# The experts' gate and up biases: from one row per turn to a table added by TensorE

## The chip, the cores and the metric

The kernel runs on one core of one Trainium2 chip. The metric is the device time of one execution in microseconds (us), the median of several runs. One execution of each kernel is also recorded with a profile; its times count from the start of the recorded span.

## What is computed

Two blocks run one after the other on 256 tokens of width 1024, all in f32. The first block (two layers of feed-forward, mixer, feed-forward) is untouched by the change. The second is a layer with attention and a mixture of 32 experts, each token going to 4 of them:

```python
h2 = rms_norm_2(x, norm2_g) * (1.0 + scale2) + shift2
# router: top 4 of 32, softmax over the four
gu = xe @ w_gate_up[e] + b_gate_up[e]          # 1024 -> 2048
g = jnp.minimum(gu[:, :1024], 7.0)
u = jnp.clip(gu[:, 1024:], -7.0, 7.0)
act = (u + 1.0) * (g * jax.nn.sigmoid(1.702 * g))
ye = act @ w_down[e] + b_down[e]               # 1024 -> 1024
x = x + gate2 * sum over the four experts of gate * ye
```

w_gate_up has 8 MB per expert and w_down 4 MB, so that the experts read 12 MB of weights 32 times.

## The kernel before

The program is written engine by engine: each phase is a block in which SyncE, GpSimd, TensorE (PE), ScalarE (ACT) and VectorE (DVE) each have their own order of instructions, joined by semaphores. Within an engine the written order holds.

**Weights.** Loads are issued by SyncE into a ring of six slots of 1 MB, in attention and before. In the expert phase six more slots join (`double`, `more`), so that a cycle is 12 slots, and transfers are of 2 MB, two slots each. Four extra slots (`once`) are used a single time, at expert 3 (APART). PE counts each slot it has consumed in `chip.used`, and SyncE waits for that count before it refills a slot (`emptied`). `landed` tells PE which count says that a slot is full.

**Experts** (`experts_phase`, from L2532). Each expert takes at most 64 tokens (CAP). The banks hold 128 rows: the 64 tokens times the first 512 columns in the lower half of the partitions, and times the last 512 columns in the upper half. Turn e on PE (`turn`) is `gate_up(e)` (eight slots, four products each, into GATE_BANK and UP_BANK, with the transposes `turn_back` after the fourth slot), `gather(e)` (tokens of expert e+1), `down(e)` (the hidden values of expert e-1 times its w_down, four slots), `turn_hidden(e)` and `scatter(e)` into four banks that stay open over all turns. Turn 0 has only gate_up and gathers, and two slots of gate_up(1) come before turn_hidden(0). Ahead of turn QUIET = 8, PE adds x and the down bias of all experts to the open banks (`add_x_and_bias`, L2741 to L2749).

**The bias before.** For each expert ScalarE issues an 8 KB DMA on its own queue (`bias_row`, L2779), which fills one partition; GpSimd spreads it over 128 partitions (`spread_bias`, L2658 to L2663). VectorE's `activate` (L2847) waits for both the products and the bias, adds it in four instructions of 64 rows each (L2852, L2857), clamps in two (L2861, L2864), multiplies by the sigmoid of ScalarE (L2797, L2866, L2869), and PE turns the result (L2727). `take_down` (L2876) scales the products of w_down.

**Attention** (`attend_phase`, L1688). PE multiplies in 24 `unit`s, whose weights ScalarE rounds (`lead`, L2009) and VectorE subtracts (`low`, L2178). ScalarE's order around the change is lead(23), evac(4), square_heads(3) (L2025), exps(3) (L2043), rms_heads(2) and (3) (L2029), take_w(2) (L2052). PE's is unit(21), pv(2) (L1864 to L1866), turn_w(3), unit(22), pv(3), unit(23), turn_heads(2). VectorE ends its part with norm_o(3), then the stt at L2396, and waits for the output product (L2401). SyncE's order is at L1735 to L1737: it waits for `x_final`, loads `norm2`, and goes on with the ring. `chip.norm_gb[:, 1, :]` is free from `x_final` on.

Of the kernel before, what the change touches and what calls it, by code (L numbers as in the profile page):

```python
# [78 lines left out]
class Chip:  # L79


    def __init__(self, nc, D, T):
        self.nc, self.D, self.T = nc, D, T
        self.KD, self.NT = D // P, T // P
        self.words = 53120
        words = 1900 + (2 * self.NT + 2) * D + self.KD * T + RING * SLOT
        self.memory = nc.alloc_sbuf_tensor("memory", [P, words], F32)
        self.psum = nc.alloc_psum_tensor("banks", [P, 8, 512], F32)
        w = Words(self.memory, 0, words)
        self.ident = w.take(P)  # L90
        self.incl = w.take(P)
# [3 lines left out]
        self.ident64, self.incl64, self.never = (w.take(64) for _ in range(3))  # L95
        self.gla_own = w.take(256)
        self.chunk_col = w.take(2)
        self.chunk_ones = w.take(2 * P).rearrange("p (c n) -> p c n", c=2)
        self.eps = w.take(4)
# [6 lines left out]
        self.xT = w.take(self.KD * T).rearrange("p (k t) -> p k t", k=self.KD)  # L106
        self.norm_gb = w.take(2 * D).rearrange("p (s d) -> p s d", s=2)
# [618 lines left out]
def mix_phase(chip, s, spent, l, loads, base, par, gamma_beta, skip, room, rows_before, mod_before):  # L726
# [72 lines left out]
    with nc.Block() as block:  # L799
# [509 lines left out]
        def _(dve):  # L1309
# [271 lines left out]
          "rank r_mm r_exp gates route_mm tables_turned gatesT")  # L1581
# [106 lines left out]
def attend_phase(chip, s, spent, routed, room, par, loads, base, n_project, b_down, mod_row, w_gate_up, w_down, rows_before):  # L1688
# [8 lines left out]
    gain2 = chip.norm_gb[:, 0, :]  # L1697
    SMALL = 4 + 8 + 4 + 3
# [16 lines left out]
    with nc.Block() as block:  # L1715
        @block.sync
        def _(sp):
# [18 lines left out]
            sp.dma_start(gain2, row(norm2)).then_inc(s["norm2"], 16)  # L1736
            chip.issue(sp, loads, base + RING + 4, OUT + RING)  # L1737
# [15 lines left out]
        def _(pool):  # L1753
# [14 lines left out]
            for m, fill in ((room.count, 0.0), (room.far, FAR)):  # L1768
                for a, n, start in ((0, P, 0), (P, 2 * P, P)):
# [8 lines left out]
                                 allow_small_or_imprecise_dtypes=True))  # L1778

# [220 lines left out]
        def _(act):  # L2000
# [120 lines left out]
            square_heads(3)  # L2121
            exps(3)
# [47 lines left out]
        def _(dve):  # L2170
# [222 lines left out]
            norm_o(3)  # L2393
            dve.wait_ge(s["norm2"], 16)
# [71 lines left out]
QUIET = 8  # L2466
ACC, GATE_BANK, UP_BANK, Y_BANK, SHARED_BANK = 0, 4, 5, 6, 7
EXPERTS = ("e_bias_row e_bias gu_read g_ready sig gated hidden sel back back_turned back_out gathered xe "
# [16 lines left out]
EXPERT_WORDS = 2048 + 1 + 2 * CAP + 256 + 256 + 3 * HALF + 2 * 8 * CAP + HALF + 3  # L2485
# [3 lines left out]
class ExpertRoom:  # L2489


    def __init__(self, chip, words, attend):
        self.double, self.more, self.once = attend.double, attend.more, attend.once
        w = Words(words, 0, EXPERT_WORDS)
        take3 = lambda a, b: w.take(a * b).rearrange("p (a b) -> p a b", a=a)
        self.bias_row, self.bias = w.take(2048), chip.norm_gb.rearrange("p s d -> p (s d)")
        self.idle = w.take(1)
# [30 lines left out]
BIAS_PIECES = 16  # L2528
# [3 lines left out]
def experts_phase(chip, s, spent, base, routed, room, gatesT, b_down, w_gate_up, b_gate_up, w_down, out):  # L2532
# [86 lines left out]
    with nc.Block() as block:  # L2619
# [36 lines left out]
        @block.gpsimd  # L2656
        def _(pool):
            def spread_bias(e):  # L2658
                pool.wait_ge(s["e_bias_row"], (e + 1) * 16)
                reach(pool, s["gu_read"], e)  # L2660

                nc.gpsimd.tensor_tensor(room.idle, chip.eps[:, 0:1], chip.eps[:, 1:2], ALU.add)
                nc.gpsimd.partition_broadcast(room.bias, room.bias_row[0:1, :]).then_inc(s["e_bias"], 1)  # L2663
# [112 lines left out]
        def _(act):  # L2776
            copy = nc.scalar.copy

            def bias_row(e):  # L2779
                reach(act, s["e_bias"], e)  # L2780
                act.dma_start(room.bias_row[0:1, :].rearrange("p (a n) -> p a n", a=BIAS_PIECES),
                              b_gate_up[0:1, ds1(e), :].rearrange("a e (k n) -> (a e) k n", k=BIAS_PIECES))\
                    .then_inc(s["e_bias_row"], 16)

# [19 lines left out]
            bias_row(0)  # L2804
            take_gathered(-1)
            bias_row(1)
# [3 lines left out]
            with act.Fori(1, NE - 1) as e:  # L2810
                take_back(e)
                bias_row(e + 1)
# [14 lines left out]
        def _(dve):  # L2827
# [18 lines left out]

            def activate(e):  # L2847
                dve.wait_ge(chip.used, taken(e, G8))
                dve.wait_ge(s["e_bias"], e + 1)
                reach(dve, s["turned"], e)  # L2850
                for h in range(2):
                    m = tt_op(room.gate[halves[h], :], psum[halves[h], GATE_BANK, :],  # L2852
                              room.bias[halves[h], h * HALF:h * HALF + HALF], ALU.add)
                m.then_inc(s["gated"], 1)
                for h in range(2):
                    c0 = D_EXPERT + h * HALF
                    m = tt_op(room.up[halves[h], :], psum[halves[h], UP_BANK, :], room.bias[halves[h], c0:c0 + HALF],  # L2857
                              ALU.add)
                    if h == 0:
                        dve.wait_ge(s["gated"], e * 2 + 1)  # L2860
                        ts(room.gate, room.gate, 7.0, None, ALU.min).then_inc(s["g_ready"], 1)  # L2861
                m.then_inc(s["gu_read"], 1)
# [4 lines left out]
                dve.wait_ge(s["gated"], e * 2 + 2)  # L2867
# [18 lines left out]
            gate2 = routed.gate2[:, 0:HALF]  # L2886
            select(-1)
# [153 lines left out]
def second_half(chip, s_attend, s_first, s_late, routed, par, loads, base, n_project, mod_row, w_gate_up, b_gate_up, w_down, b_down, out, rows_before):  # L3041

    nc = chip.nc
    with nc.sbuf_tensor("attend_words", [P, ATTEND_WORDS], F32) as words:
        with nc.sbuf_tensor("attend_parts", [P, PARTS_WORDS], F32R) as parts:
            pass
        with nc.sbuf_tensor("attend_later", [P, PARTS_WORDS], F32) as later:
            room = AttendRoom(chip, parts, later, words, routed)
            attend_phase(chip, s_attend, s_first.span(), routed, room, par, loads, base, n_project, b_down, mod_row, w_gate_up, w_down, rows_before)
# [86 lines left out]
```

## Time and profile before

| | us |
|---|---|
| median of 3 runs | 2338.59 (2338.49 to 2339.9) |
| the profiled execution | 2338.61 |
| its span | 2336.9 |
| PE busy | 2237.7 (96%) |
| DVE busy | 1050.3 (45%) |
| ACT busy | 598.0 (26%) |
| POOL busy | 173.3 (7%) |

Attention runs from about 1220 to 1377 us, the expert phase from there to the end. The page gives busy times by engine, the span in 40 slices, the DMA queues and the costliest groups. A group's line names the line of the code, the engine, the operation, what it writes and reads, and how often. PE products in plain f32 stand there with two records each, products of rounded operands with one. The chain of waits follows the work back from the last instruction; a timeline has each instruction's start and length, and in brackets the idle time before it and what ended that. DMA queue 1 is SyncE's, queue 10 ScalarE's.

### The profile page before, as it was taken

The numbers are of one execution on the slowest core, as the hardware profiler recorded it, in microseconds if no ns is written. First come the engines' busy times: TensorE is split into PE (matmuls) and PEld (weight loads), VectorE is DVE, ScalarE is ACT, GpSimd is POOL, SyncE is SP. The second block draws the span as 40 slices with busy tenths as digits, with TensorE's granted clock in tenths as the row PEclk, the third lists the DMA queues.
The fourth block names the chain that finished last, engine by engine and source line by source line (L and its number), as shares of the span: only waits on it lengthen the run. The fifth ranks groups of instructions, "written<-read, shape, count | busy, mean of one in ns | idle before, by whom it ended". The sixth has DMA issues, their size and how long they took to land. (4 is left out here: it accounts for less than half of the span.)

```text
span 2336.9 us, 31286 instructions
## 1 busy us (share of the span) xinstructions
PE 2237.7 (96%) x12797; PEld 1408.6 (60%) x12798; DVE 1050.3 (45%) x1497; ACT 598.0 (26%) x809; POOL 173.3 (7%) x194
## 2 busy tenths in 40 slices
PE   7999989999999998999999999999999999999998
PEld 6886875788788776668877654444443333333333
DVE  4563573665566447556558642222222222222222
ACT  4442331543443322244436521000000000000000
POOL 5000020000000001000010001000100000000000
PEclk9999999999999999999999999999999999999999
DMA  8763311687387352158635659999999999999996
GB/s 276 246 237 105 124 74 45 226 271 244 108 282 248 116 164 77 38 168 281 235 128 168 226 225 423 399 425 411 424 426 425 425 428 423 407 417 407 412 425 254
DMA packets 189376, 633.61 MB, mean 271 GB/s; under 512 B 29568, under 2 KB 125840, under 8 KB 163392
## 3 DMA queue, kind: packets, MB, share of 16 engines
q1 hardware_dynamic: 189216, 631.96, 70.7%
q8 instruction: 73, 1.20, 0.2%
q10 hardware_dynamic: 64, 0.26, 0.0%
q14 instruction: 23, 0.19, 0.0%
HBM read 631.12 MB, written 1.07 MB: 271 GB/s over the span
## 5 line engine op out<-in xcount | busy, mean ns | idle before, releaser
L403 PE MATMUL banks<-ffn_room 128*128 128x512 f32 x1920 | 453.7, 392 | 0.0
L403 PEld LDWEIGHTS banks<-ffn_room 128*128 128x128 f32 x1920 | 357.5, 188 | 72.8
L520 DVE TENSOR_TENSOR ffn_room<-memory,ffn_room 128x2048 fp32r<-128x2048 f32 x124 | 280.9, 2292 | 99.2 <-ACT ffn_room L480 99.1
L2852 DVE TENSOR_TENSOR attend_words<-banks,memory 64x512 f32<-64x512 f32 x64 | 44.2, 690 | 529.6 <-PE banks L2682 529.2
L480 ACT CAST ffn_room<-memory 128x2048 fp32r<-128x2048 f32 x124 | 232.0, 1903 | 69.0 <-PE banks L421 61.9
L421 PE MATMUL banks<-ffn_room 128*128 128x512 f32 x1056 | 248.2, 390 | 0.3
L421 PEld LDWEIGHTS banks<-ffn_room 128*128 128x128 f32 x1056 | 197.6, 188 | 42.8 <-DVE ffn_room L559 2.1
L2682 PE MATMUL banks<-attend_later,attend_words 128*64 128x512 f32 x960 | 217.7, 595 | 3.1 <-DMA attend_later<-in_w_gate_up 2.3
L2698 PE MATMUL banks<-memory,attend_words 128*64 128x512 f32 x952 | 211.4, 595 | 0.0
L2682 PE MATMUL banks<-attend_words 128*64 128x512 f32 x496 | 122.6, 640 | 28.5 <-DMA attend_words<-in_w_gate_up 28.3
L2682 PEld LDWEIGHTS banks<-attend_later,attend_words 128*64 128x64 f32 x960 | 66.1, 136 | 129.5 <-issue 122.4
L2698 PEld LDWEIGHTS banks<-memory,attend_words 128*64 128x64 f32 x952 | 65.0, 135 | 121.1 <-issue 117.6
L2717 PEld LDWEIGHTS banks<-attend_words,memory 128*128 128x128 f32 x1056 | 120.5, 192 | 26.0 <-issue 26.0
L2682 PE MATMUL banks<-memory,attend_words 128*64 128x512 f32 x592 | 134.2, 597 | 0.7 <-ACT attend_words L2793 0.7
L2717 PE MATMUL banks<-attend_words,memory 128*128 128x64 f32 x1056 | 124.8, 276 | 0.0
L486 ACT ACTIVATE memory<-banks 128x256 f32<-128x256 f32 x88 | 33.8, 385 | 342.6 <-PE banks L403 318.8
L2793 ACT COPY attend_words<-banks 128x512 f32<-128x512 f32 x33 | 19.4, 587 | 392.1 <-PE banks L2717 392.1
L535 DVE TENSOR_TENSOR memory<-memory,banks 128x256 f32<-128x256 f32 x88 | 36.8, 418 | 176.7 <-ACT memory L486 166.0
L2682 PEld LDWEIGHTS banks<-attend_words 128*64 128x64 f32 x496 | 36.3, 146 | 112.1 <-issue 67.3
L869 PE MATMUL banks<-memory 128*128 128x400 f32 (+1 forms) x256 | 101.1, 549 | 1.2 <-PEq L363 1.2
L2663 POOL PARTITION_BROADCAST memory<-attend_words x32 | 73.9, 2309 | 289.3 <-issue 289.3
L2682 PEld LDWEIGHTS banks<-memory,attend_words 128*64 128x64 f32 x592 | 39.3, 135 | 89.2 <-issue 88.4
(434 smaller groups left out, 2398.9 us busy)
## 6 DMA issues: line engine op xcount, KB each, us to landing
memory<-in_ffn_w SPq DMA_DIRECT2D x132, 1024.0 KB, 7.5
memory<-in_w_down SPq DMA_DIRECT2D x58, 2048.0 KB, 23.2
attend_later<-in_w_gate_up SPq DMA_DIRECT2D x58, 2048.0 KB, 24.3
memory<-in_w_gate_up SPq DMA_DIRECT2D x34, 2048.0 KB, 22.0
attend_words<-in_w_gate_up SPq DMA_DIRECT2D x30, 2048.0 KB, 24.7
memory<-in_w_in SPq DMA_DIRECT2D x32, 1024.0 KB, 6.3
memory<-in_w_ada SPq DMA_DIRECT2D x32, 768.0 KB, 5.6
memory<-in_w_out SPq DMA_DIRECT2D x12, 1024.0 KB, 4.9
```

The costliest lines, as they stand in the source:

```text
L403: m = nc.tensor.matmul(psum[:, GU + tt, :], x_parts[:, xp, k, tt * P:tt * P + P], rows, start=(n == 0), stop=(n == 3 * KD - 1))
L421: return nc.tensor.matmul(psum[:, 2 * tt + h, :], hidden_parts[:, ft % 2, hp, tt, c, :], rows[:, c, h * 512:h * 512 + 512], start=(ft == 0 ...
L480: nc.scalar.copy(split_place(i)[0], chip.ring[:, chip.slot(base + i), :]).then_inc(s["lead"], 1)
L486: nc.scalar.activation(gate[:, tt, :], psum[:, GU + tt, 0:FT], ACT.Silu).then_inc(s["gate"], 1)
L520: tt_op(b, chip.ring[:, chip.slot(base + i), :], a.bitcast(F32), ALU.subtract).then_inc(chip.used, 1)
L535: tt_op(hidden[:, tt, :], gate[:, tt, :], psum[:, GU + tt, FT:2 * FT], ALU.mult)\
L869: m = mm(psum[:, n % 2, 0:cols], chip.xT[:, k, half * P:half * P + P], slots[k // 4][:, k % 4, :], start=(k == 0), stop=(k == KD - 1))
L2663: nc.gpsimd.partition_broadcast(room.bias, room.bias_row[0:1, :]).then_inc(s["e_bias"], 1)
L2682: m = mm(psum[halves[h], bank, :], room.xeT[:, k, :], rows[:, c0 + h * HALF:c0 + h * HALF + HALF], start=(k == 0), stop=(k == G8 - 1))
L2698: m = mm(psum[halves[h], Y_BANK, :], room.actT[:, k, :], rows[:, c * D_EXPERT + h * HALF:c * D_EXPERT + h * HALF + HALF], start=(k == 0), ...
L2717: m = mm(psum[:, SHARED_BANK, k * CAP:k * CAP + CAP], routed.h2[:, tt, k * P:k * P + P], room.sel[:, tt, :], start=(tt == 0), stop=(tt == ...
L2852: m = tt_op(room.gate[halves[h], :], psum[halves[h], GATE_BANK, :], room.bias[halves[h], h * HALF:h * HALF + HALF], ALU.add)
```

## The change

The biases of all experts are loaded once, in attention, into one table of 128 partitions and 2 x 512 columns: partitions 0 to 31 hold the first half of the gate and up columns of experts 0 to 31, 32 to 63 the second half, and 64 to 127 the same again. ScalarE rounds the upper copy to the type f32r (`bias_table`, partitions 0 to 63) and the lower likewise (`bias_low`), and VectorE puts the remainder of the rounding into partitions 64 to 127. GpSimd prepares two small masks. In the experts VectorE makes a 128x128 selector for each expert (`pick`), and PE adds the bias by one product with that selector into each of the two banks, ahead of the weight products, which then add on. The per-turn row, the broadcast and the four additions are gone; VectorE clamps straight from the banks. QUIET becomes 18, so that x and the down bias are added ahead of turn 18.

```diff
-QUIET = 8
+QUIET = 18
@@ attend_phase, SyncE
             sp.dma_start(gain2, row(norm2)).then_inc(s["norm2"], 16)
+            for r in range(0, P, NE):
+                sp.dma_start(bias_raw[r:r + NE, :].rearrange("e (g n) -> e g n", g=2),
+                             b_gate_up[0:1, :, :].rearrange("a e (g h n) -> (a e) h g n", g=2, h=2)[:, (r // NE) % 2, :, :])\
+                    .then_inc(s["bias"], 16)
             chip.issue(sp, loads, base + RING + 4, OUT + RING)
@@ attend_phase, GpSimd, after its last step
+            chain(nc.gpsimd.memset(chip.bias_rows[:, NE:NE + 1], 0.0))
+            chain(nc.gpsimd.memset(chip.bias_halves, 0.0))
+            for i in range(P // NE):
+                chain(nc.gpsimd.memset(chip.bias_halves[i * NE:i * NE + NE, CAP * (i % 2):CAP * (i % 2) + CAP], 1.0))
...
@@ attend_phase, ScalarE
             square_heads(3)
+            act.wait_ge(s["bias"], 16 * (P // NE))
+            act.wait_ge(s["bias_made"], 1)
+            copy(chip.bias_table[halves[0], :], bias_raw[halves[0], :]).then_inc(s["bias_lead"], 1)
+            act.wait_ge(s["bias_lead"], 1)
+            copy(chip.bias_low[halves[1], :], bias_raw[halves[1], :]).then_inc(s["bias_lead"], 1)
             exps(3)
@@ attend_phase, VectorE
             norm_o(3)
+            dve.wait_ge(s["bias_lead"], 2)
+            tt_op(chip.bias_table[halves[1], :], bias_raw[halves[1], :], chip.bias_low[halves[1], :].bitcast(F32), ALU.subtract)
             dve.wait_ge(s["norm2"], 16)
@@ experts_phase, GpSimd
-            def spread_bias(e):
...
-            spread_bias(0)
-            with pool.Fori(1, NE) as e:
-                spread_bias(e)
@@ experts_phase, TensorE, gate_up
                 reach(pe, s["gu_read"], e)
+                if tiles[0] == 0:
+                    pe.wait_ge(s["picked"], e + 1)
+                    for g, bank in enumerate((GATE_BANK, UP_BANK)):
+                        mm(psum[:, bank, :], room.pick, room.bias[:, g, :],
+                           start=True, stop=True)
                 for k in tiles:
...
-                                   rows[:, c0 + h * HALF:c0 + h * HALF + HALF], start=(k == 0), stop=(k == G8 - 1))
+                                   rows[:, c0 + h * HALF:c0 + h * HALF + HALF], start=False, stop=True,
+                                   skip_group_check=True)
@@ experts_phase, ScalarE
-            bias_row(0)
             take_gathered(-1)
-            bias_row(1)
...
                 take_back(e)
-                bias_row(e + 1)
                 take_gathered(e)
@@ experts_phase, VectorE
+            def pick(e):
+
+                ts(room.pick, room.halves, room.rows[:, ds1(e)], None, ALU.mult).then_inc(s["picked"], 1)
+
             def activate(e):
                 dve.wait_ge(chip.used, taken(e, G8))
-                dve.wait_ge(s["e_bias"], e + 1)
                 reach(dve, s["turned"], e)
-                for h in range(2):
-                    m = tt_op(room.gate[halves[h], :], psum[halves[h], GATE_BANK, :],
-                              room.bias[halves[h], h * HALF:h * HALF + HALF], ALU.add)
...
-                ts(room.up, room.up, 7.0, -7.0, ALU.min, ALU.max)
+                ts(room.gate, psum[:, GATE_BANK, :], 7.0, None, ALU.min).then_inc(s["g_ready"], 1)
+                ts(room.up, psum[:, UP_BANK, :], 7.0, -7.0, ALU.min, ALU.max).then_inc(s["gu_read"], 1)
+                pick(e + 1)
                 dve.wait_ge(s["gu_read"], e + 1)
...
+            pick(0)
             select(-1)
```

The table, the selector and the masks lie in memory that the first block's mixer used for constants and, for the table, next to `norm_gb`; nothing else moves.

## Rows read from the trace of the kernel before

**Rows 1.** The page: busy times of the engines, and the DMA row in 40 slices.
```profile
PE 2237.7 (96%) x12797; PEld 1408.6 (60%) x12798; DVE 1050.3 (45%) x1497; ACT 598.0 (26%) x809; POOL 173.3 (7%) x194
...
DMA  8763311687387352158635659999999999999996
```

**Rows 2.** Table of stretches: span, busy of PE, PEld, DVE, ACT, POOL, clock, DMA, GB/s.
```profile
1600.00:1620.00 20.00, 20.00 (x76) 6.29 (x78) 0.00 (x0) 0.37 (x1) 0.00 (x0) 1.00 0.94 383
...
1700.00:1720.00 20.00, 19.79 (x108) 9.00 (x106) 9.05 (x13) 1.71 (x3) 2.66 (x2) 1.00 1.01 431
...
2000.00:2304.00 304.00, 286.45 (x1420) 116.21 (x1420) 75.91 (x130) 20.84 (x40) 26.63 (x20) 0.98 1.00 414
```

**Rows 3.** Chain of waits in order of time: start us, us, what.
```profile
1542.03 7.02 PE banks L2682 x32
...
1567.22 0.70 DVE attend_words L2876
...
1569.96 7.02 PE banks L2682 x32
...
1597.88 8.43 PE banks L2749 x16
...
2000.34 5.38 PE banks L2682 x16
...
2304.83 3.65 PE banks L2682 x16
```

**Rows 4.** Timeline of SyncE, turn 3 to 4.
```profile
1469.27 3.76 SPq L2633 DMA_DIRECT2D memory<-in_w_down  x2
1489.96 0.36 SPq L2633 DMA_DIRECT2D memory<-in_w_gate_up  x1
```

**Rows 5.** DMA view, 1485 to 1493: busy tenths in 40 slices.
```profile
DMA  9939937935335313113113113113099960098199
```

**Rows 6.** DMA view of 1525.3 to 1526.3, then issues of three later stretches.
```profile
q10 hardware_dynamic: 1, 0.01, 2.0%
...
attend_words<-in_b_gate_up ACTq DMA_DIRECT2D x10, 8.0 KB
...
attend_words<-in_b_gate_up ACTq DMA_DIRECT2D x8, 8.0 KB
...
memory<-in_w_down SPq DMA_DIRECT2D x20, 2048.0 KB, 24.3
...
attend_words<-in_b_gate_up ACTq DMA_DIRECT2D x9, 8.0 KB
```

**Rows 7.** PE's waits from 1731 to 2305: in total, times, longest.
```profile
PE banks L2682 <- DMA attend_words<-in_w_gate_up: 28.3, 16, 2.8
```

**Rows 8.** Timeline of PE in turn 0.
```profile
1405.19 0.66 PE L2727 MATMUL banks<-memory,attend_words 128*128 128x128 f32 x4 [0.16 <-DVE attend_words L2869]
```

**Rows 9.** Rounded and plain f32 products of 512 columns: page's group, then timeline.
```profile
L403 PE MATMUL banks<-ffn_room 128*128 128x512 f32 x1920 | 453.7, 392 | 0.0
...
1317.88 3.68 PE L1894 MATMUL banks<-memory 128*128 128x512 f32 x8
```

**Rows 10.** Timelines of SyncE and ScalarE in attention.
```profile
1256.95 2.51 SPq L132 DMA_DIRECT2D memory<-in_w_in  x2
...
1286.56 1.04 ACT L2009 CAST attend_parts<-memory 128x1024 fp32r<-128x1024 f32 x1 [1.97 <-PE banks L1812]
```

**Rows 11.** Timelines of ScalarE, PE and VectorE around the added steps.
```profile
1295.45 1.05 ACT L2009 CAST attend_parts<-memory 128x1024 fp32r<-128x1024 f32 x1 [0.70 <-PE banks L1812]
...
1301.99 0.77 ACT L2052 COPY attend_words<-banks 128x768 f32<-128x768 f32 x1
...
1302.82 0.43 PE L1864 MATMUL banks<-attend_words 128*128 128x64 f32 x2 [1.29 <-ACT attend_words L2052]
...
1357.10 1.22 DVE L2401 TENSOR_TENSOR memory<-attend_later,banks 128x1024 f32<-128x1024 f32 x1 [5.51 <-PE banks L1894]
```

**Rows 12.** Table of stretches (columns as in rows 2).
```profile
1302.00:1306.00 4.00, 3.18 (x20) 3.09 (x21) 2.48 (x10) 1.22 (x3) 0.00 (x0) 0.80 0.34 139
```

More of the change, by code:

```diff
@@ L86, in __init__ @@
         words = 1900 + (2 * self.NT + 2) * D + self.KD * T + RING * SLOT
+        at = -(-nc.sbuf_base // 32) * 32
         self.memory = nc.alloc_sbuf_tensor("memory", [P, words], F32)
+        self.rounded = nc.alloc_sbuf_tensor_at("memory_rounded", [P, words], F32R, offset=at)
         self.psum = nc.alloc_psum_tensor("banks", [P, 8, 512], F32)
@@ L90, in __init__ @@
         self.ident = w.take(P)
+        self.bias_low = self.rounded[:, w.at:w.at + D]
         self.incl = w.take(P)
@@ L95, in __init__ @@
         self.ident64, self.incl64, self.never = (w.take(64) for _ in range(3))
+        self.bias_pick = self.rounded[:, w.at + 64:w.at + 192]
         self.gla_own = w.take(256)
@@ L106, in __init__ @@
         self.xT = w.take(self.KD * T).rearrange("p (k t) -> p k t", k=self.KD)
+        self.bias_table = self.rounded[:, w.at + D:w.at + 2 * D]
         self.norm_gb = w.take(2 * D).rearrange("p (s d) -> p s d", s=2)
@@ L1580 @@
           "d_ss d_rms d_out mix_turned mixT mixed x_new x_turned n_ss n_rms hT_first hT_last cst_mm shifted "
-          "rank r_mm r_exp gates route_mm tables_turned gatesT")
+          "rank r_mm r_exp gates route_mm tables_turned gatesT bias bias_lead bias_made")
 class Routed:
@@ L1685, with attend_phase @@
 PIECES = ((0, P), (P, WIDE))
-def attend_phase(chip, s, spent, routed, room, par, loads, base, n_project, b_down, mod_row, w_gate_up, w_down, rows_before):
+def attend_phase(chip, s, spent, routed, room, par, loads, base, n_project, b_down, mod_row, w_gate_up, b_gate_up, w_down, rows_before):
     nc, D, KD, NT = chip.nc, chip.D, chip.KD, chip.NT
@@ L1697, in attend_phase @@
     gain2 = chip.norm_gb[:, 0, :]
+    bias_raw = chip.norm_gb[:, 1, :]
     SMALL = 4 + 8 + 4 + 3
@@ L2465 @@
 CAP = 64
-QUIET = 8
+QUIET = 18
 ACC, GATE_BANK, UP_BANK, Y_BANK, SHARED_BANK = 0, 4, 5, 6, 7
-EXPERTS = ("e_bias_row e_bias gu_read g_ready sig gated hidden sel back back_turned back_out gathered xe "
+EXPERTS = ("picked gu_read g_ready sig gated hidden sel back back_turned back_out gathered xe "
            "turned act ye scat down_bias tables scat_first first_rows last_rows")
@@ L2495, in __init__ @@
         take3 = lambda a, b: w.take(a * b).rearrange("p (a b) -> p a b", a=a)
-        self.bias_row, self.bias = w.take(2048), chip.norm_gb.rearrange("p s d -> p (s d)")
-        self.idle = w.take(1)
+        self.bias = chip.bias_table.rearrange("p (g n) -> p g n", g=2)
+        self.pick, self.halves, self.rows = chip.bias_pick, chip.bias_halves, chip.bias_rows
         self.sel = take3(chip.NT, CAP)
@@ L2657, in _ @@
         def _(pool):
-            def spread_bias(e):
[L2659 to L2663, printed above, removed]
             pool.sem_clear(spent)
-            spread_bias(0)
-            with pool.Fori(1, NE) as e:
-                spread_bias(e)
         @block.tensor
@@ L2777, in _ @@
             copy = nc.scalar.copy
[L2779 to L2783, printed above, removed]
             def take_back(e):
@@ L2845, in select_back @@
                 m.then_inc(s["back"], 1)
+            def pick(e):
+                ts(room.pick, room.halves, room.rows[:, ds1(e)], None, ALU.mult).then_inc(s["picked"], 1)
             def activate(e):
                 dve.wait_ge(chip.used, taken(e, G8))
-                dve.wait_ge(s["e_bias"], e + 1)
                 reach(dve, s["turned"], e)
-                for h in range(2):
-                    m = tt_op(room.gate[halves[h], :], psum[halves[h], GATE_BANK, :],
-                              room.bias[halves[h], h * HALF:h * HALF + HALF], ALU.add)
[L2854 to L2862, printed above, removed]
+                ts(room.gate, psum[:, GATE_BANK, :], 7.0, None, ALU.min).then_inc(s["g_ready"], 1)
+                ts(room.up, psum[:, UP_BANK, :], 7.0, -7.0, ALU.min, ALU.max).then_inc(s["gu_read"], 1)
+                pick(e + 1)
                 dve.wait_ge(s["gu_read"], e + 1)
-                ts(room.up, room.up, 7.0, -7.0, ALU.min, ALU.max)
                 dve.wait_ge(s["sig"], e + 1)
                 tt_op(room.gate, room.gate, room.sig, ALU.mult).then_inc(s["gated"], 1)
-                dve.wait_ge(s["gated"], e * 2 + 2)
+                dve.wait_ge(s["gated"], e + 1)
                 by_row = lambda v: v.rearrange("p (n c) -> p c n", c=4)
@@ L3048, in second_half @@
             room = AttendRoom(chip, parts, later, words, routed)
-            attend_phase(chip, s_attend, s_first.span(), routed, room, par, loads, base, n_project, b_down, mod_row, w_gate_up, w_down, rows_before)
+            attend_phase(chip, s_attend, s_first.span(), routed, room, par, loads, base, n_project, b_down, mod_row, w_gate_up, b_gate_up, w_down, rows_before)
             experts_phase(chip, s_first, s_late.span(), base + n_project + N_OUT, routed, ExpertRoom(chip, words, room), room.gatesT, room.b_down,
```

5 lines of the change are left out of this document (3 added, 2 removed).

## The prediction

> **What bounds the kernel now.** I read the page first. PE is busy 96% of the span, and the DMA row in tenths stands at 9 from slice 24 on, so from about 1400 us two resources are full at once [rows 1]. The table of stretches tells them apart. From 1700 to 1720 PE is busy 19.79 of 20 us; from 2000 to 2304 it is busy 286.45 of 304 us, so it waits, and the sixteen DMA engines carry 414 to 431 GB/s all along, with shares of 0.99 to 1.01 [rows 2]. The chain of waits has the same turning point. A turn of the expert loop takes 27.93 us while PE leads it (1542.03 to 1569.96); late in the loop the waits for weights at 2000.34 and 2304.83 are ten turns apart, 30.45 us each [rows 3]. An expert's weights are 12.58 MB, which at 426 GB/s take 29.5 us. PE is thus faster per turn than the transfers, and the stock of landed slots is used up on the way.
>
> So the end is set by a sum of three: when the stream of weights can start, what it loses when slots come free too late, and how fast it runs. Two places of loss are seen. At 1489.96 SyncE issues a load after a gap of some 17 us (the two before it went out from 1469.27 on) [rows 4]: ring slots are short there, since the four extra ones are used once, and the load waits for PE's second product group of turn 4. The DMA row of 1485 to 1493 (slices of 0.2 us) falls from 9 to 3 and then 1 before it rises at 1490.8 [rows 5]. I read that as follows: the sixteen engines don't run dry together; the first ends at about 1486, the last not before 1491, so after 100 us of streaming they are 4 to 5 us apart, and a transfer has landed only when its slowest engine is done. The other place is 1600 to 1620, at 383 GB/s instead of 426 [rows 2], behind the 8.43 us of x and down bias [rows 3].
>
> **Part 1, the bias rows go.** In 1490 to 1757, 1757 to 2000 and 2000 to 2304 the ACT queue issues 10, 8 and 9 rows of 8 KB, 27 in all [rows 6]. In the microsecond from 1525.3 queue 10 has one data packet, which takes 2.0% of sixteen engines' time: 0.02 x 16 = 0.32 us on one engine. At 426 / 16 = 26.6 GB/s the 8192 bytes would take 0.31 us, so the whole row lies on one engine [rows 6]. By mean throughput that is 0.02 us a turn and nothing. But if that engine is the slowest, each turn loses 0.31 us, 27 x 0.31 = 8.4 us. The ends are 0 and 8.4; I take nine tenths, 7.6, nearer to the upper end, since the spread of the engines at 1485 to 1493 shows that one engine decides and this one alone has work added.
> The row shows one packet on one engine, not which engine nor whether it is always the same. The Trainium skill (DMA: Bandwidth & Descriptors, section Why a DMA increments its semaphore by 16 and not by 1) states that a DMA from the scalar queue which can't be divided goes to the lowest-numbered engine; by that all rows add up on one engine and the upper end holds; were they dealt round, the saving would be 0.5 us. No view of the profile numbers the engines, so the trace neither agrees nor disagrees.
>
> GpSimd's broadcast and VectorE's four 64-row additions per turn go too. In the late turns neither is in the chain, where VectorE appears only with take_down's 0.70 us [rows 3]; PE's waits late in the loop are for transfers (28.3 us in 16) [rows 7]. Worth: 0. In turn 0 VectorE's product of the gates does end a wait of 0.16 us of PE, which the next part uses up [rows 8].
>
> **Part 2, two products per expert.** Full-width single-record products of this shape in the feed-forward took 453.7 us for 1920, 0.236 each [rows 9]. So 2 x 0.236 = 0.47 us a turn on PE, at the start of gate_up, before the products that free slots. A turn of PE becomes 28.4 us, still under the transfers' 30. The upper end: the plain f32 calls of the output projection are two records each, 3.68 us for 8 records, 0.92 a call [rows 9], 1.84 us a turn if the rounded type did not hold; the change reads both operands through the rounded view, so I take 0.47. A gain is excluded: the weight products stay the same. Up to the load of 1489.96 five pairs come (turns 0 to 4): 5 x 0.47 = 2.35, less the 0.16 in turn 0, is 2.2 us later. There the last engine is running dry just as the new load begins to move (about 1 us after its issue), so up to about half a microsecond of lateness is free; I charge 1.7 (1.2 to 2.2). After the restart the pairs cost nothing, PE having 1.6 us a turn to spare over the transfers; that cover gone, each would cost 0.47. In turn 31 the pair runs while PE would wait for the last weights. VectorE's pick of 128 columns lies behind the two clamps, long before the next expert's products.
>
> **Part 3, x and down bias from turn 8 to turn 18.** At turn 8 the stock is thin and the engines with a lead run dry: 383 for 426 GB/s over 20 us is 2.0 us of mean throughput [rows 2]. The slowest engine hardly stops, for the reason read at 1485 to 1493. Value 0, ends -2.0 and 0. At turn 18 the same 8.43 us meet queued transfers worth some 24 us (issue to landing in the last window is 24.3 us [rows 6]), so nothing stops; PE is then late by 8.4 and regains 30 - 28.4 = 1.6 us a turn, in six turns of the thirteen left. Cost 0; if PE's turn were near 30, it would not be regained.
>
> **Part 4, the table in attention.** SyncE issues four loads of 128 KB behind norm2's. The next load in its queue is a w_in slot, issued from 1256.95 on, whose first reader is ScalarE's cast at 1286.56 [rows 10], so about 2.5 us of issue is covered; 0.5 MB is 1.2 us of transfer in a stage with the queues half empty [rows 1]. GpSimd's masks are small and stand after its last counted step; queue and engine are idle there. Cost 0.
> ScalarE is given two copies of 64x1024 between square_heads(3) and exps(3), at 1298.4. A cast of 1024 columns takes 1.05 us, for 128 rows and I take the same for 64 [rows 11]; two with the wait between them 2.1. Queued behind are exps(3), rms_heads and take_w(2) (L2052, 1301.99), and for take_w(2) PE waits already: 1.29 us of idleness before its product at 1302.82 [rows 11]. So all of it goes to the path: +2.1, from there through pv(2), units 22 and 23 and turn_heads, which stand in PE's order. From below, 1.0 if ScalarE's own idle time took one copy; from above 3.4, if PE's longer pause costs it more time at half clock: from 1302 to 1306 the granted clock was 0.80 already [rows 12].
> VectorE's subtraction of 64x1024 (1.2 us) lies in the 5.51 us that it idles before 1357.10 [rows 11]: 0.
>
> **Sum.** Against the profiled execution's own 2338.61 (span 2336.9 and 1.7 around it; the median of the runs is 2338.59, the same): -7.6 + 1.7 + 0 + 2.1 = -3.8, so 2334.8 us. About 0.2%, 4.7 us, is what a measurement can tell from no change; the forecast lies just within.
>
> **Rivals.**
> A, the rows' engine isn't the slowest, or rows are dealt round: 27 x 0.02 = 0.5 instead of 7.6 gives 2338.6 - 0.5 + 1.7 + 2.1 = 2341.9. For it: the mean throughput hardly notices the rows. Against: the engines' spread. 0.12.
> B, all of the row's price comes back, and the pause at turn 8 counts too: -8.4 - 2.0 + 1.7 + 2.1 = 2332.0; with quieter neighbours on the engines somewhat less. For it: the drop to 383 GB/s is plain in the windows. 0.37.
> C, slower: the products cost as plain f32, 1.84 a turn. Then the restart comes 5 x 1.84 - 0.16 - 0.5 = 8.5 us late, PE's turn is 29.8, and the 8.43 us at turn 18 are regained at 0.3 a turn, 4 of them in thirteen turns, 4.4 left: 2338.6 + 2.1 + 8.5 + 4.4 - 7.6 = 2346.0. It decides from a PE turn of about 29.5 us on, a pair of 1.6. With a longer half-clock stretch in attention (+1.3) on top of rival A it would reach 2343.2 in another way. Together 0.13.
> D, the change doesn't do what it says for the path, since every removed step is covered: that is A.
> The forecast has 0.38.
>
> **How the numbers follow.** Faster by over 0.2% (under 2333.9): B, 0.37, and 0.03 of the forecast's lower edge: 0.40. Slower (over 2343.3): C, 0.13. Same: the rest, 0.47. The range goes from B's 2332.0 less the quieter neighbours and ScalarE's lower end (3 us) to A with its clock cost: 2329 to 2343.5.
>
> **What the profile would show.** Right: no queue 10 and no broadcast; the chain's late turns at 30.1 to 30.2 us; SyncE's load of 1489.96 at 1494.3; PE's pause before L1864 at 3.4 instead of 1.29; PE turns of 28.4 before the waits begin; no dip at 1600 to 1620; the tail behind the last weights still 32 us. Late turns unchanged at 30.4 would speak for A; pairs at over 1.6 us for C. The prediction would be wrong if packets of the weights themselves changed speed once the ACT queue is silent, which no row of before can show.

## The result, and the profile after

The changed kernel takes 2315.24 us (median of six runs, 2313.12 to 2317.9) where the kernel before takes 2338.54 (six runs, 2336.37 to 2339.9): a ratio of 0.9902, 95% interval 0.9889 to 0.9914. That is 23.3 us, or 1.0%, off; 3.8 had been forecast, and the result lies well under the range of 2329 to 2343.5. The profiled execution of after took 2313.12 us with a span of 2311.4. One execution of the kernel before, among the 13 beside group 2 below, took 4608.56 us, and the ratios leave it out.

The page of after, answering to [rows 1]:
```profile
PE 2246.0 (97%) x12861; PEld 1418.9 (61%) x12862; DVE 973.5 (42%) x1403; ACT 600.2 (26%) x811; POOL 89.7 (4%) x137
...
DMA  8773311677386343139745559899999999999998
```
Its table of stretches (columns as in rows 2), the experts' chain, and the chain's shares by engine over the whole span:
```profile
1600.00:1620.00 20.00, 19.79 (x101) 8.31 (x101) 2.69 (x8) 0.96 (x2) 0.00 (x0) 1.00 1.01 430
...
2000.00:2304.00 304.00, 301.70 (x1528) 125.02 (x1527) 52.27 (x105) 22.81 (x44) 0.00 (x0) 1.00 0.98 419
```
```profile
1602.29 0.66 PE banks L2692 x2
1602.95 7.02 PE banks L2699 x32
...
1631.54 7.02 PE banks L2699 x32
```
```profile
PE 39%; DVE 1%; issue 0%; ACT 0%
```
PE is busy 301.70 of 304 us late in the loop, where it was 286.45 [rows 2]. A turn takes 1631.54 - 1602.95 = 28.59 us (28.58 in the mean of ten) with the pair of products (L2692) in it, and no transfer is in the chain. PE's waits from 1731 to 2305 have one line left where a transfer's 28.3 us stood [rows 7]:
```profile
PE banks L2755 <- DVE attend_words L2878: 4.1, 20, 0.2
```
So the bound has changed hands: before, the transfers set a late turn (30.4 us), now PE does (28.58). The stretch 1600 to 1620 moves 430 GB/s instead of 383.

Attention of after, answering to rows 11 and 12, timelines of ScalarE and PE, then a stretch:
```profile
1294.39 1.03 ACT L2140 CAST memory_rounded<-memory 64x1024 fp32r<-64x1024 f32 x1
1295.45 1.05 ACT L2142 CAST memory_rounded<-memory 64x1024 fp32r<-64x1024 f32 x1
```
```profile
1300.95 0.69 PE L1880 MATMUL banks<-attend_words 128*128 128x64 f32 x2 [3.44 <-ACT attend_words L2068]
```
```profile
1302.00:1306.00 4.00, 4.00 (x18) 3.81 (x18) 2.13 (x7) 0.80 (x1) 0.00 (x0) 0.50 0.02 4
```
The two copies cost PE 3.44 - 1.29 = 2.15 us of waiting, and the granted clock behind it is 0.50 (1.2 GHz) where it was 0.80.

One more difference stands at the very start, where the change touches nothing. GpSimd and PE in the first microseconds, of before and then of after:
```profile
11.73 0.28 POOL L633 TENSOR_SCALAR_AFFINE_SELECT memory<-memory 128x128 f32<-128x128 f32 x1 [10.69 <-issue]
12.16 3.65 PE L653 MATMUL banks<-memory 128*128 128x128 f32 x16 [12.16 <-POOL memory L633]
```
```profile
1.29 0.29 POOL L639 TENSOR_SCALAR_AFFINE_SELECT memory<-memory 128x128 f32<-128x128 f32 x1 [0.24 <-POOL memory L638]
6.20 3.67 PE L659 MATMUL banks<-memory 128*128 128x128 f32 x16 [6.20 <-DMA memory<-in_x]
```
Before, GpSimd idles 10.69 us for nothing that the profile shows ("issue"), and PE's first product waits for it. The same kind of gap stands in each turn of the expert loop of before, between the idle addition and the broadcast (timeline of GpSimd, then its waits from 1377 on):
```profile
1652.02 0.35 POOL L2662 TENSOR_TENSOR attend_words<-memory 128x1 f32<-128x1 f32 x1 [15.48 <-DVE attend_words L2857]
1662.16 2.30 POOL L2663 PARTITION_BROADCAST memory<-attend_words  x1 [9.79 <-issue]
```
```profile
POOL memory L2663 <- issue: 289.3, 32, 10.8
```
32 gaps, 289.3 us, 9.0 us each. The addition waits for VectorE before it starts; between it and the broadcast no semaphore stands, and still 9 us pass. These rows carry the explanation below.

### The profile page after: what moved, and what is told of

It reads as the page before. It is cut to its first block and busy times, and to the rows that moved or that the text cites. A ratio compares the mean times of both kernels' runs of the same rounds, so it can differ in the third digit from the quotient of the medians.

```text
span 2311.4 us, 30925 instructions
## 1 busy us (share of the span) xinstructions
PE 2246.0 (97%) x12861; PEld 1418.9 (61%) x12862; DVE 973.5 (42%) x1403; ACT 600.2 (26%) x811; POOL 89.7 (4%) x137
## 5 line engine op out<-in xcount | busy, mean ns | idle before, releaser
L2863 DVE TENSOR_SCALAR attend_words<-banks 128x512 f32<-128x512 f32 x32 | 22.1, 692 | 518.7 <-PE banks L2699 518.7
L2699 PE MATMUL banks<-attend_words 128*64 128x512 f32 x496 | 111.8, 592 | 0.0
L2800 ACT COPY attend_words<-banks 128x256 f32<-128x256 f32 x32 | 11.9, 373 | 305.6 <-PE banks L2726 305.6
L871 PE MATMUL banks<-memory 128*128 128x256 f32 x384 | 85.4, 379 | 0.0
```

The source lines that it names most:

```text
L871: m = mm(psum[:, n % 2, c * 256:c * 256 + 256], slots[k // 4][:, k % 4, cc:cc + P], chip.xT[:, k, :], start=(k == 0), stop=(k == KD - 1))
L2699: m = mm(psum[halves[h], bank, :], room.xeT[:, k, :], rows[:, c0 + h * HALF:c0 + h * HALF + HALF], start=False, stop=True, skip_group_chec ...
```

## The experiments

Four theories stood: rows (8 KB on one DMA engine each turn), writing (what GpSimd's broadcast puts into memory, 1 MB a turn, disturbs the transfers), switching (the idle addition and the broadcast are taken to be different code on GpSimd, and each change of code disturbs the transfers; no view shows the code itself, so "change of code" stands below for an addition followed by a broadcast, or a broadcast by an addition), and the move of the 8.43 us of x and down bias. The kernels ran in four groups, each beside the kernel before, whose medians were 2337.43 (16 runs), 2339.16 (13), 2336.59 (15) and 2338.18 us (15); differences of 1 us between groups mean nothing. The ratios are taken over all runs and not from the two medians, and can differ from their quotient by as much as 1 us.

**Group 1: parts undone one by one, in the kernel before.** The row loaded for expert 0 alone (both later calls of `bias_row` gone, the broadcast kept); the broadcast for expert 0 alone:
```diff
-                pool.wait_ge(s["e_bias_row"], (e + 1) * 16)
+                pool.wait_ge(s["e_bias_row"], 16)
...
-                bias_row(e + 1)
```


> The kernel before, with ScalarE's bias row loaded for expert 0 alone; the broadcasts, VectorE's additions and turn 8 stay (all experts but the first get the wrong bias). Rows theory (the 8 KB rows on ScalarE's queue are what slows the weight stream, by 0.31 us a turn on one engine and by slowed packets of the others): late turns fall from 30.4 to 29.3 us, the time to 2312 to 2320. Broadcast theory (GpSimd's broadcast disturbs the transfers): 2330 to 2337, the 8.4 us of the rows at most. Turn-8 theory (the pause at turn 8 is what costs): 2336 to 2339.

```diff
-                nc.gpsimd.tensor_tensor(room.idle, chip.eps[:, 0:1], chip.eps[:, 1:2], ALU.add)
-                nc.gpsimd.partition_broadcast(room.bias, room.bias_row[0:1, :]).then_inc(s["e_bias"], 1)
+                m = nc.gpsimd.tensor_tensor(room.idle, chip.eps[:, 0:1], chip.eps[:, 1:2], ALU.add)
+                if isinstance(e, int) and e == 0:
+                    m = nc.gpsimd.partition_broadcast(room.bias, room.bias_row[0:1, :])
+                m.then_inc(s["e_bias"], 1)
```


> The kernel before, with GpSimd's broadcast for expert 0 alone, the rows still loaded each turn (all experts but the first get the wrong bias). Rows theory: 2336 to 2339, late turns 30.4 us. Broadcast theory: late turns 29.5 us, 2312 to 2322. Turn-8 theory: 2336 to 2339.

Both edits together, and `QUIET` set to 18 with nothing else changed:

> The kernel before with neither rows nor broadcasts after expert 0 (all experts but the first get the wrong bias). Rows and broadcast theories alike: late turns 29.3 us, 2308 to 2318, and equal to whichever of the two single removals is the cause. If the layout of memory or the products are the cause, 2330 to 2339.

> The kernel before with QUIET = 18 alone, output complete. Rows and broadcast theories: 0 to 2 us faster, 2336 to 2339, since the slowest DMA engine hardly stops at turn 8 and the late turns stay at 30.4 us. Turn-8 theory: 2315 to 2330.

| kernel | us | against the before of its group | ratio, 95% |
|---|---|---|---|
| no rows | 2329.06 | -8.4 | 0.9966 (0.9955 to 0.9978) |
| no broadcasts | 2314.23 | -23.2 | 0.9905 (0.9889 to 0.9922) |
| neither | 2309.08 | -28.4 | 0.9881 (0.9864 to 0.9897) |
| bias at turn 18 | 2337.07 | -0.4 | 0.9999 (0.9989 to 1.0009) |

The move is worth nothing, though its stretch 1600 to 1620 shows 428 GB/s instead of 383. The broadcasts alone are worth as much as the whole change. The rows bring more than the broadcast theory had left for them (2330 to 2337) and far less than the rows theory asked for (2312 to 2320). The late turns tell the same by the turn; each pair of lines is the chain of one kernel, nine turns apart: before, no rows, no broadcasts, neither.
```profile
2005.86 24.77 DMA attend_words<-in_w_gate_up
...
2279.07 25.71 DMA attend_words<-in_w_gate_up
```
```profile
1968.21 25.51 DMA attend_words<-in_w_gate_up
...
2239.14 26.62 DMA attend_words<-in_w_gate_up
```
```profile
1987.28 25.62 DMA attend_words<-in_w_gate_up
...
2254.23 25.48 DMA attend_words<-in_w_gate_up
```
```profile
1984.27 25.50 DMA attend_words<-in_w_gate_up
...
2248.59 25.48 DMA attend_words<-in_w_gate_up
```
30.36, 30.10, 29.66 and 29.37 us a turn. The row is worth 0.26 (beside broadcasts) or 0.29 (without); the broadcast 0.70 or 0.73. The figures with broadcasts are the rough ones: single turns of before scatter there from 28.2 to 32.7 us (13 turns from 1882.34 on make 30.52 in the mean), while without rows and broadcasts each is within 0.03 of 29.37.

**Group 2: what of the broadcast costs.** First, the kernel before with the idle addition left out and GpSimd's loop written out, so that 32 broadcasts stand one behind the other:
```diff
-                nc.gpsimd.tensor_tensor(room.idle, chip.eps[:, 0:1], chip.eps[:, 1:2], ALU.add)
...
-            spread_bias(0)
-            with pool.Fori(1, NE) as e:
+            for e in range(NE):
                 spread_bias(e)
```


> The kernel before, complete, with GpSimd's one-element addition ahead of each broadcast left out and its loop written out, so that GpSimd runs nothing but broadcasts. Switching theory (what slows the packets is the preparation of some 9 us between that addition and the broadcast, in which GpSimd changes from built-in to loaded code): the gap before the broadcasts is gone, late turns are 29.6 to 29.7 us and the time is that of the kernel without broadcasts, 2312 to 2318. Writing theory (the broadcast's own 1 MB of writes into SBUF slows the packets): late turns 30.4 us, 2335 to 2339.

2319.82 us (2318.15 to 2320.08), ratio 0.9923 (0.9905 to 0.9941). The gaps are gone from GpSimd's waits, which are:
```profile
POOL memory L2662 <- DVE attend_words L2855: 798.9, 31, 33.9
POOL memory L2662 <- issue: 139.5, 1, 139.5
```
Late turns take 29.69 us by its chain, as with no broadcasts at all:
```profile
1993.28 25.82 DMA attend_words<-in_w_gate_up
...
2260.47 25.51 DMA attend_words<-in_w_gate_up
```
The median is 5.6 us longer than without broadcasts all the same, and above the 2312 to 2318 of the switching theory; the turns don't account for it.

Then the other way round, added to the changed kernel: in each turn the addition and a broadcast of 16 columns (8 KB written), or two additions of 128x1024 on GpSimd (1 MB written, no change of code), or the row on ScalarE's queue.
```diff
+                nc.gpsimd.tensor_tensor(room.idle, chip.eps[:, 0:1], chip.eps[:, 1:2], ALU.add)
+                nc.gpsimd.partition_broadcast(room.spare[:, 0:16], chip.x[0:1, 0, 0:16]).then_inc(s["e_bias"], 1)
```


> The kernel after, output complete, with one addition and a broadcast of only 16 columns (8 KB instead of 1 MB) per expert on GpSimd, whose result nobody uses. Switching theory: the packets are slowed as in the kernel before, late turns 30.1 us and waits for transfers come back: 2328 to 2336. Writing theory: no effect, 2313 to 2318.

```diff
+                for h in range(2):
+                    reach(pool, s["e_bias"], e * 2 + h)
+                    nc.gpsimd.tensor_tensor(room.spare, chip.x[:, h, :], chip.x[:, 1 - h, :], ALU.add).then_inc(s["e_bias"], 1)
```


> The kernel after, output complete, with two additions of 128x1024 per expert on GpSimd (1 MB of writes, no broadcast), whose result nobody uses. Switching theory: no effect, 2313 to 2318. Writing theory: transfers slowed as before, 2328 to 2336. A third, that GpSimd's use of the port it shares with VectorE delays VectorE enough to reach PE: PE's waits for L2878 grow from 7.2 us in all.

```diff
+                act.dma_start(room.bias_row[0:1, :].rearrange("p (a n) -> p a n", a=16),
+                              b_gate_up[0:1, ds1(e), :].rearrange("a e (k n) -> (a e) k n", k=16))\
+                    .then_inc(s["e_bias_row"], 16)
```


> The kernel after, output complete, with the 8 KB row per expert on ScalarE's queue put back, its data unused. Row theory (0.31 us a turn on the slowest engine): the transfers need 29.6 us a turn instead of 29.3 while PE needs 28.6, so part of it shows: 0 to 4 us slower, 2315 to 2319. If the row alone slowed all packets, 2325 or more.

The small broadcast took the changed kernel back to 2336.62 us (2333.84 to 2339.97; ratio to before 0.9994, 0.9984 to 1.0004), with the gaps back in GpSimd's waits:
```profile
POOL memory L2686 <- issue: 315.2, 32, 11.2
```
The large additions left it at 2315.02 (2314.61 to 2317.71), and PE's waits for VectorE's `take_down` stayed at 7.2 us in all, so the third theory, of the port, fails too. The row made it 2320.89 (2319.9 to 2324.04), beyond the 2315 to 2319 expected. So the writing costs nothing measurable, additions and broadcasts in turn cost 21 us, and the row 5.6.

**Group 3: the start, the layout of the row, the copies.** The 5.6 us that the unswitched kernel had too much point at the start: every kernel whose last GpSimd instruction is a broadcast shows the gap of some 10 us at its start. If an execution starts with the code that the one before it left, an addition behind the last broadcast should end that.
```diff
                 spread_bias(e)
+            pool.wait_ge(s["e_bias"], NE)
+            nc.gpsimd.tensor_tensor(room.idle, chip.eps[:, 0:1], chip.eps[:, 1:2], ALU.add)
```


> The kernel before, complete, with one more addition of one column on GpSimd behind the last broadcast, so that GpSimd ends the program on built-in code instead of broadcast code. In the profile of before GpSimd's L633 starts at 11.73 us, 10.69 us late for nothing that the profile shows, and TensorE's first product waits for it until 12.16; in the profile of the changed kernel the same instruction starts at 1.29 and the first product at 6.2, for a transfer. Theory S (an execution begins with the code that the last one left, and must bring the built-in code back): L633 starts at about 1.3, the first product at about 6.2, attention 4 to 5 us earlier, and the time is about 2334 (2332 to 2335.5), with the 31 switches of the experts' loop left as they are. Rival N (the late start is chance, or belongs to the program's length): 2337 to 2340, L633 at about 11.7.

> The kernel before, complete, without the idle addition in each turn of GpSimd's stream (its loop written out, so that 32 broadcasts follow each other with no built-in code between them) and with one addition behind the last of them. With the broadcasts alone it took 2319.8 us and its first product started at 12.22. Theory S (the first experiment of this call): the first product at about 6.2 and 2314 to 2316. If so, all 32 broadcasts of 8 KB and all 32 row loads are there, and what is gone of before is only the changing of code: 1 + 31 times. It would be about as fast as the changed kernel, so the products, the attention table and the moved biases bring nothing by themselves beside it. Rival N: 2319 to 2321.

In both the first select is at 1.52 us and the first product at 6.05 and 5.90, here for the kernel before with the addition:
```profile
1.52 0.29 POOL L633 TENSOR_SCALAR_AFFINE_SELECT memory<-memory 128x128 f32<-128x128 f32 x1 [0.49 <-POOL memory L632]
...
6.05 3.47 PE L653 MATMUL banks<-memory 128*128 128x128 f32 x16 [6.05 <-DMA memory<-in_x]
```
The unswitched kernel went from 2319.82 to 2314.4 (2312.81 to 2317.9), as expected. The kernel before went from 2336.59 only to 2335.62 (ratio 0.9997, 0.9988 to 1.0006; some -2.8 to +1.4 us): the instructions moved as expected, the time did not.

The copies of the table moved behind `take_w(3)` (the diff is shortened), and the row of group 2 laid out over 16 partitions:
```diff
             exps(3)
             rms_heads(2)
             rms_heads(3)
             take_w(2)
             take_w(3)
+            (the two copies of the bias table)
```


> The changed kernel, complete, with the copies of the bias table on ScalarE in attention moved behind the exps and scalings of heads 2 and 3, away from the wait that TensorE has at L1880. In the profile of the changed kernel that wait is 3.44 us where it was 1.29, and the products behind it run at a granted clock of 0.50 for a while. Theory: both go, 2.1 us of waiting and about 1.3 us of clock: 2311 to 2313. Rival (ScalarE is late again for the next reader of the same chain, so the copies only move the wait): 2314 to 2316.

> The changed kernel with the 8 KB row of gate and up biases loaded again each turn on ScalarE's queue and read by nobody, but laid out over 16 partitions, 512 bytes each. With the row as one partition it took 2320.9 (5.6 us over the changed kernel), its packets lying on few of the 16 DMA engines. Theory E (the row costs by what it adds to the slowest engine, 0.3 us a turn): spread out, it adds a sixteenth to each, and the time is 2315 to 2317. Rival Q (a second queue beside the weights costs by itself, whatever its layout): 2320 to 2322.

Moved, PE's wait before L1880 is the old 1.29 us again (timeline of PE):
```profile
1299.01 0.43 PE L1880 MATMUL banks<-attend_words 128*128 128x64 f32 x2 [1.29 <-ACT attend_words L2068]
```
The experts' first products stand 2.9 us earlier (1380.18 for 1383.08), and the time is 2310.91 us (2307.89 to 2313.91; ratio to before 0.9889, 0.9874 to 0.9904), the shortest complete kernel of this study. The spread row took 2316.92 (2316.06 to 2319.95) where the row on one partition took 2320.89. By their ratios the two are 3 us apart and the intervals overlap (0.9933, 0.9914 to 0.9953, and 0.9920, 0.9907 to 0.9934); the chains are clearer: the last turns that wait for transfers take 29.61 us with the row on one partition and 29.37 with the spread one, which is the figure without any row. The pages have queue 10 so, one partition first:
```profile
q10 hardware_dynamic: 64, 0.26, 0.0%
```
```profile
q10 hardware_dynamic: 1024, 0.26, 0.1%
```
That is 2 and 32 packets a row. The code cuts the row on one partition into 16 pieces too (`a=16` in the diff of group 2), and it went out undivided all the same. So what the row costs is mostly that it lies on one engine.

**Group 4: how the terms add.**

> The changed kernel, complete, with one addition of one column and one broadcast of 16 columns on GpSimd at the start of the experts' stage and nothing on GpSimd behind them, so that the program ends on broadcast code and changes code once in the loop. Theory S (the next execution's start pays for that): GpSimd's first affine select at about 12 us instead of 1.29, TensorE's first product at about 12.2 instead of 6.2, attention 4 to 5 us later, and, since TensorE and not the transfers bounds this kernel's experts, the whole of it at the end: 2319 to 2321. Rival N (a late start is made good later, as the 2335.6 of the kernel before with one more addition at its end would have it): 2315 to 2317, the first product late all the same.

> The changed kernel, complete, with the addition and the 16-column broadcast in each turn, and one more addition behind the last, so that 31 changes of code stay in the loop and none is left for the next start. Without the last addition it took 2336.6. Theory S as a plain sum: 4.5 to 5.5 us less, 2331 to 2332.5. Theory S with a floor (when the changes of code hold the transfers back, an earlier start of TensorE is mostly lost in waiting for them): 2334 to 2336.5, and TensorE waits more for transfers than without the addition.

> The changed kernel without the two products a turn that add the gate and up biases (these biases are left out of the result; the table is still loaded and copied in attention). In the profile of the changed kernel a turn of TensorE takes 28.58 us, and 27.93 in the profile of before. Theory P (TensorE's turns set the end): 0.65 us a turn less, 2315.2 minus 20 would be 2295. Theory F (the transfers move 428 to 429 GB/s, their most, and stand just behind TensorE, so that with TensorE faster they set the end at 29.3 to 29.4 us a turn): 2310 to 2314, TensorE waiting for transfers in the last ten turns.

One broadcast at the start of the experts and no addition behind it: 2318.1 us (2315.91 to 2320.5), 2.9 over the changed kernel, between what the two theories gave. Its start is late like that of before:
```profile
11.57 0.28 POOL L639 TENSOR_SCALAR_AFFINE_SELECT memory<-memory 128x128 f32<-128x128 f32 x1 [10.54 <-issue]
12.00 3.65 PE L659 MATMUL banks<-memory 128*128 128x128 f32 x16 [12.00 <-POOL memory L639]
```
Addition and broadcast in every turn and a start without the gap: 2335.56 (2332.96 to 2340.45), so the loop's changes alone are 20.3 us over the changed kernel, and the start brings 1.1 beside them. That is the time of the theory with a floor, but not its reason: PE waits no longer for transfers than without the last addition (18.1 and 18.3 us in all), and attention begins only 0.8 us earlier (1216.17 for 1217.00). Without the products: 2311.07 (2310.72 to 2312.23), 4.2 off instead of 20; the chain's late turns are
```profile
2046.26 25.49 DMA attend_words<-in_w_gate_up
...
2251.81 25.50 DMA attend_words<-in_w_gate_up
```
seven turns of 29.36 us. That is the transfers' floor for this loop, with nothing else on the engines. The changed kernel, at 28.58 a turn, runs on the stock of landed slots and comes to its end just before the stock does: in the kernel with the copies moved, which is 2.9 us earlier in the loop, one wait for a transfer (at 2254.65) is back in the chain.

## Why the prediction was wrong, step by step

**The step that failed** is the sentence "Worth: 0" on GpSimd's broadcast in part 1. It asked whether broadcast or addition was in the chain of waits; neither was, and that was right. The wrong step was to take from this that nothing else on the chip paid for them. The trace of before had 32 gaps of 9 us between an addition and a broadcast with no semaphore between them, and one of 10.69 us at the start, and none was asked about. Taken away, they are worth, in the loop, 20.3 us (the changed kernel with and without them) and 0.70 to 0.73 us a turn (the late turns), and at the start 1 to 5.4 us by kernel. The prediction's last sentence named the outcome (the weights' packets change speed) but held the ACT queue responsible; with the rows gone and the broadcasts kept it was 8.4 us, not 23.
That the alternation, and not the writing, slows the transfers is shown by the 8 KB broadcast with an addition (+21) against 1 MB of additions (0), and by the broadcasts without additions (late turns 29.69). The traces also show where in a turn it happens. Mean GB/s over the 22 broadcasts from 1625 to 2280, in stretches counted from each broadcast's start:

| kernel | 6 to 2 us before | 2 before to 6 behind | 6 to 10 behind | 10 to 16 behind |
|---|---|---|---|---|
| before | 407 | 427 | 389 | 428 |
| no rows | 421 | 429 | 401 | 428 |
| broadcasts without additions | 428 | 428 | 429 | 428 |

So there are two dips. One lies in the 9 us gap between addition and broadcast; the other behind the broadcast, where GpSimd waits for VectorE and no gap is seen. That the way back has a gap of its own shows only where an addition follows a broadcast at once: in the kernel before with one more addition at the end, that addition starts after 11.2 us of "issue". The sixteen engines are busy in the dips (shares of 0.99 to 1.00), so the packets take longer there. By the bytes missing in the two dips, the loss is about 0.56 us a turn in before and 0.33 in the kernel without rows (estimates from the table), of the 0.70 to 0.73 that the turns show. What it is on the chip that slows the packets isn't shown: the page counts no more data on any queue with the alternation than without. The Trainium skill (GPSIMD Engine Reference, section 2.1, Instruction dispatch) says that new code can be brought in to GpSimd by DMA at run time and that the first call to freshly loaded code pays about 6 us that no instruction shows. The gaps are of that kind, and here they measure 9.0 us in the mean, before every broadcast that follows an addition; that these two instructions differ in this way is inferred, not seen.

**The rows** were costed at 7.6, ends 0 and 8.4. Undone alone they are worth 8.4 (interval 5.1 to 10.5; late turns 30.10, where 30.1 to 30.2 had been named), added to the changed kernel 5.6. The reasoning by one slow engine held: the row spread over 16 costs 1.7. The rows add up, at 0.26 to 0.29 us a turn for a packet of 0.31, so they fall on one and the same engine; the Trainium skill's rule of the lowest-numbered engine (DMA: Bandwidth & Descriptors, section Why a DMA increments its semaphore by 16 and not by 1) fits that, though no view shows which engine it is. Rival A is out.

**The products** were put at 0.47 us a turn; the pair takes 0.66 in the chain and a turn grew from 27.93 to 28.58, 0.65. The rounded type held (rival C is out), but the row it was taken from has 0.236 a product and these take 0.33. The larger slip is "after the restart the pairs cost nothing": with turns of transfers at 30.4 that was so; at 29.36 the pair brings PE close to the transfers, and it costs 4.2 us (1.7 had been charged); it does not cost 31 x 0.65 = 20, since without it the transfers set the end. The restart load came at 1492.41 for 1494.3: attention began 4.0 us earlier, its clock took 1.3 and five pairs 0.9 more than was charged.

**The move of x and down bias**: 0, and 0 was measured (-0.4, interval -2.6 to +2.1). The dip to 383 GB/s goes and brings nothing.

**Attention** was put at +2.1, upper end 3.4. PE's pause was 3.44 as said. From GpSimd's first mark of attention to the experts' first products it is 1383.08 - 1214.43 = 168.65 us, before 1383.02 - 1218.45 = 164.57; less the new pair's 0.66 that is +3.4, the upper end. The 1.3 beyond the pause is put down to the lower clock behind it; with the copies moved both are gone (164.85).

**The start** wasn't in the sum at all. Attention begins at 1214.43 instead of 1218.45. Over all profiled kernels it begins at 1217.0 to 1223.3, mean 1219.8, in the six whose last GpSimd instruction is a broadcast, and at 1214.4 to 1218.8, mean 1215.9, in the eleven others: 3.9 us of the 6 that the first product gains.

Put together: without rows and broadcasts, -28.4 us; the products give back 4.2, and with about 1 for the rest -23.3 is what remains. That 1 is a remainder and was not measured by itself; in the changed kernel, where PE sets the end, moving the copies alone gave 2.4 to 4.3 us. The single terms (8.4 and 23.2) add to 3.2 more than their 28.4 together, which is within their intervals.

**What stays open** is what in the change between addition and broadcast slows the packets, and how much of the early start reaches the end while transfers set it: 1.0 and 1.1 us in the two kernels with changes in the loop, 2.9 and 5.4 in those without, each known to about 2 us.

## What to carry to other kernels

Read the idle time of every engine that ends on "issue", also of one that is 7% busy and never in the chain: it may go with slower transfers, and in a stage where transfers set the pace that is paid there. If GpSimd must do additions and broadcasts, keep all of one kind together, and let the program end on the kind that it begins with (that last step alone brought between 1 and 5.4 us here). And before valuing a removed cost, write down the next floor: here PE's turn (28.58 us) and the transfers' (29.36) lay so near that of 20 us given back on PE only 4.2 reached the end.

## What was not expected of the hardware

- Additions and broadcasts alternating on GpSimd: 9.0 us of idleness before each broadcast, and 0.70 to 0.73 us a turn lost by 12.58 MB of weights on another queue, in two dips of some 4 us; 20 us over the loop.
- The last GpSimd instruction of a program decides how it starts: behind a broadcast the first product is at 12.2 us instead of 6.0, and attention begins 3.9 us later in the mean. That one execution leaves this to the next is the reading; each trace holds a single execution.
- A row of 8 KB as one packet costs 5.6 us over 31 turns, the same bytes over 16 partitions 1.7.
